# Low parts of the feed-forward weights, made for two units in one subtraction

## The reference

```python
h = h + mix
u = rms_norm(h, norm_mlp_g[i])
h = h + jnp.square(jax.nn.relu(u @ mlp_w1[i])) @ mlp_w2[i]
gate = jax.nn.sigmoid(rms_norm(h, ple_norm_g[i]) @ ple_w_gate[i])
h = h + gate * (p[i] @ ple_w_proj[i])
```

## Time and profile before

| | us |
|---|---|
| median of 3 runs | 1205.45 |
| lowest, highest run | 1203.81, 1205.74 |
| span of the profiled execution | 1202.4 |
| TensorE busy in it | 1190.7 (99%) |
| VectorE busy in it | 735.9 (61%) |
| ScalarE busy in it | 590.9 (49%) |

### The profile page before, as it was taken

One profiled execution on the slowest core, in us unless ns is written; L12 is line 12 of the kernel. 1 busy time (PEld: TensorE's weight loads), 2 busy tenths in 40 slices (PEclk: granted clock), 3 DMA queues, 4 the chain that ended last, 5 costly groups with the idle time before them and its releaser, 6 DMA issues.

```text
span 1202.4 us, 14118 instructions
## 1 busy us (share of the span) xinstructions
PE 1190.7 (99%) x5468; PEld 987.3 (82%) x5468; DVE 735.9 (61%) x977; ACT 590.9 (49%) x808; POOL 71.2 (6%) x63
## 2 busy tenths in 40 slices
PE   8999999999999999999999999999999999999998
PEld 6887788888888888888888888888888888888886
DVE  5677746778766647554465555556555557576554
ACT  6655444666566544443444433445433445455443
POOL 1000000000000011100011100012000012000000
PEclk9999999999999999999999999999999999999999
DMA  9777764333358667766568665677755676786661
GB/s 336 278 214 248 221 200 137 119 106 117 108 167 267 216 208 228 257 225 194 194 212 259 226 213 192 193 247 237 235 193 194 210 240 212 253 263 199 214 205 54
DMA packets 110980, 249.25 MB, mean 207 GB/s; under 512 B 9665, under 2 KB 55745, under 8 KB 110913
## 3 DMA queue, kind: packets, MB, share of 16 engines
q1 hardware_dynamic: 110768, 248.34, 63.6%
q10 hardware_dynamic: 144, 0.01, 0.0%
HBM read 233.63 MB, written 14.68 MB: 207 GB/s over the span
## 4 chain that ended last, share of the span: by engine, by line
PE 94%; DVE 2%; ACT 1%; DMA 1%; SPq 1%; issue 0%; ACTq 0%
PE acc L1495 88%; PE sc L1638 1%; DMA x_raw<-in_x_cols_dram 1%; DVE w_split L997 1%; ACT s L734 1%; PE sc L1603 0%; PE tr L1555 0%; PE tr L1544 0%; PE sc L1544 0%; PE tr L1691 0%; PE tr L1690 0%; PE acc L1527 0%; ACT q_split L719 0%; PE tr L1673 0%; PE tr L1667 0%
## 5 line engine op out<-in xcount | busy, mean ns | idle before, releaser
L997 DVE TENSOR_TENSOR w_split<-w_raw,w_split 128x1024 fp32r<-128x1024 f32 x408 | 506.0, 1249 | 382.0 <-ACT w_split L632 381.4
L632 ACT ACTIVATE w_split<-w_raw 128x1024 fp32r<-128x1024 f32 x408 | 428.5, 1058 | 414.5 <-PE acc L1495 410.8
L1495 PE MATMUL acc<-w_split,a_hi 128*128 128x512 f32 x1916 | 594.7, 392 | 4.7 <-DVE w_split L997 3.1
L1495 PE MATMUL acc<-w_split,b_split 128*128 128x512 f32 x1920 | 440.9, 390 | 0.0
L1495 PEld LDWEIGHTS acc<-w_split,a_hi 128*128 128x128 f32 x1916 | 356.2, 188 | 81.1 <-issue 4.9
L1495 PEld LDWEIGHTS acc<-w_split,b_split 128*128 128x128 f32 x1920 | 359.4, 188 | 74.0
L1495 PE MATMUL acc<-w_split,a_lo 128*128 128x512 f32 x958 | 373.2, 390 | 0.0
L1495 PEld LDWEIGHTS acc<-w_split,a_lo 128*128 128x128 f32 x958 | 179.8, 188 | 37.9
L591 POOL TENSOR_TENSOR stage<-stage 128x512 f32<-128x512 f32 x32 | 49.5, 1567 | 560.3 <-ACT stage L640 560.3
L734 ACT ACTIVATE s<-s,nmx,q_scale 128x128 f32<-128x128 f32 (+1 forms) x64 | 34.2, 539 | 7.8 <-DVE nmx L1175 7.4
L640 ACT ACTIVATE stage<-acc,rstd 128x512 f32<-128x512 f32 x48 | 30.2, 679 | 10.1 <-PE acc L1495 9.7
(11 more groups left out here) (184 smaller groups left out, 516.3 us busy)
## 6 DMA issues: line engine op xcount, KB each, us to landing
w_raw<-in_mlp_w_units_dram SPq DMA_DIRECT2D x256, 512.0 KB, 4.3
w_raw<-in_nsa_w_in_units_dram SPq DMA_DIRECT2D x76, 512.0 KB, 4.4
w_raw<-in_nsa_w_out_units_dram SPq DMA_DIRECT2D x32, 512.0 KB, 4.3
w_raw<-in_ple_w_gate_units_dram SPq DMA_DIRECT2D x32, 512.0 KB, 4.3
turn_dram<-s SPq DMA_DIRECT2D x52, 128.0 KB, 4.1
turn_dram<-junk SPq DMA_DIRECT2D x44, 128.0 KB, 4.2
v_slc<-turn_dram SPq DMA_DIRECT2D x22, 256.0 KB, 4.3
v_win<-turn_dram SPq DMA_DIRECT2D x22, 256.0 KB, 4.2
```

What stands on the lines that cost most here:

```text
L632: nc.scalar.activation(w_hi[:, u % SPLIT], w_raw[:, u % RAW], ACT.Copy).then_inc(hi_done, 1)
L997: nc.vector.tensor_tensor(w_lo[:, u % SPLIT], w_raw[:, u % RAW], f32(w_hi[:, u % SPLIT]), ALU.subtract).then_inc(lo_done, 1)
L1495: last = nc.tensor.matmul(acc[c % 2][t][:], xs[:, kt, toks], ws[:, u % SPLIT, m * NW:(m + 1) * NW], start=(kt == 0 and n == 0), stop=(kt = ...
```

## The change

A second generator, `split_lo_wide`, takes the place of `split_lo` in chunks 1 to 5 of all four quarters and in chunks 6 to 8 of the first three. At every even k it waits until the high parts of units k and k+1 are both done, subtracts both in one instruction of 2048 columns (the two slots lie side by side), and counts `lo_done` up by 2. At odd k it issues nothing. The other work stands behind the same k as before. Everything else, the last chunks of the last quarter among it, keeps `split_lo`.

```diff
+            def split_lo_wide(first, n, i=0):
+
+                for k in range(n):
+                    u = first + k
+                    if k % 2 == 0:
+                        dve.wait_ge(hi_done, u + 2 + 8 * UPC * i)
+                        s, r = slice(u % SPLIT, u % SPLIT + 2), slice(u % RAW, u % RAW + 2)
+                        nc.vector.tensor_tensor(w_lo[:, s], w_raw[:, r], f32(w_hi[:, s]),
+                                                ALU.subtract).then_inc(lo_done, 2)
                     yield k
 
@@ -1415,20 +1426,20 @@
             def hidden_chunks(i):
 
                 for j in range(1, 5):
-                    for k in split_lo(FIRST[C_MLP + j], UPC, i):
+                    for k in split_lo_wide(FIRST[C_MLP + j], UPC, i):
                         if k == 2 and j > 1:
                             turned_hidden(j - 2, i)
                         if k == 4:
                             dve.wait_ge(squared, TT * j + 4 * TT * i)
                             turn_blocks(T_HID + j - 1, lambda t: stage[:, t], i)
-                for k in split_lo(FIRST[C_MLP + 5], UPC, i):
+                for k in split_lo_wide(FIRST[C_MLP + 5], UPC, i):
                     if k == 2:
                         turned_hidden(3, i)
 
             for q in range(QUARTERS - 1):
                 hidden_chunks(q)
                 for j in range(6, 9):
-                    for k in split_lo(FIRST[C_MLP + j], UPC, q):
+                    for k in split_lo_wide(FIRST[C_MLP + j], UPC, q):
                         if j == 6 and k in (1, 2):
                             add_to_h(C_MLP + 3 + k, k - 1, q)
```

More of the change, by code:

```diff
@@ L999, in split_lo @@
                     yield k
+            def split_lo_wide(first, n, i=0):
[6 more added lines that the diff above has]
+                                                ALU.subtract).then_inc(lo_done, 2)
+                    yield k
             def transposed_lo(r, hi, lo, kt0, gain, i=0, banks=(0, 1)):
```

## The result

| | us |
|---|---|
| before, median of the runs | 1205.37 |
| after, median of the runs | 1226.79 |
| after / before | 1.0186 (95%: 1.0172 to 1.0199) |
| span of the profiled execution, before and after | 1202.4, 1225.9 |

A forecast was written before the change was run, and what follows sets the result against it. TensorE was taken as the bound, with no waits to win back. Its new stalls summed to 4.10 + 4e a quarter, 6.5 us with e = 0.6, 26 us in four quarters: 1205.45 + 26 = 1231.5 us, range 1212 to 1250.

The forecast's parts named there:

- The bound: Feed-forward part: TensorE has no slack and waits for nobody, VectorE has slack; TensorE busy 1190.7 of 1202.4 us.
- the 17 us of the working: VectorE's relief from 116 wide subtractions replacing 232: 0.15 us a pair, 17 us in all, none reaching the end.
- The pair's duration and slack: Wide subtraction takes about 2.30 us; low part ready at 6.11 against limit 7.72, leaving 1.6 us in an undisturbed pair.
- A - 6.31: Chunks 2 to 4: TensorE's stall at units 2 and 3, the block's return time in the chunk less 6.31 us.
- A - 7.85: Chunk 5, without evacuation or squaring: TensorE's stall is the block's return time in the chunk less 7.85 us.
- T: Moment SP sends the hidden block away to DRAM; forecast 18.32 us into chunk 1, 2.0 later than before.
- A to T: Chunks 2 to 4: from the block's return from DRAM to the next block's sending away, forecast 11.70 us.
- e: Lengthening of T to A because loads come in pairs; taken as 0.6 us, between near 0 and 1.6.
- T to A: Block's trip through DRAM, from sending away to return; 10.58 to 13.18 us before, forecast to lengthen by e.
- the prediction's own sign of being wrong: One of three signs: the block's return does not move though T, its sending away, does.
- Where the longest stall is: TensorE's longest idle time at unit 2 was forecast in chunk 2 of each quarter, about 3 us.
- a rival with 16 falls: TensorE's clock halves for one unit at each of 16 stalls: 43.5 us more, 1275 us; chance 0.04.

## Why the prediction was right

- **The bound.** TensorE was full in this stretch and VectorE was not: right. VectorE lost 30.5 us of work and the time rose. The relief was larger than the 17 us of the working, because squaring and subtracting now overlap less: GpSimd's squares fell from 1567 to 1042 ns on average, and 10 us of the relief lie in the subtractions for the turned blocks, which fell from 29.6 to 19.4 us in all.
- **The pair's duration and slack.** 2.29 undisturbed (2.30 forecast), 2.63 to 2.64 beside the squares (2.71). Pairs 0 and 1, 4 and 5, 6 and 7 and all of chunks 1 and 6 to 8 never stall, as forecast.
- **The limit.** A - 6.31 held: 1.08 by it, 1.12 in the stall shown, and within some 0.1 us in the others of chunks 2 to 4 (with the clock's 2.5 taken off the longest). A - 7.85 for chunk 5 gives 0.73 and 0.79 where the trace has 0.86 and 0.93.
- **The block's departure.** T was forecast at 18.32 in chunk 1 and is 613.33 - 595.03 = 18.30. A to T was forecast at 11.70 and is 11.43; VectorE's instructions overlap by some 0.08 at three places, which the sum leaves out, and that makes most of the difference.
- **The term that was mis-sized: e, and its spread.** T to A, by chunk from which the block comes: 12.19, 11.06, 10.91, 11.47 before, 11.16, 11.59, 12.43, 12.88 after. The mean e is 0.60, the value taken, and by the table above it lies on the way back (5.3 to 6.0). That the mean hit is in part luck, since 0.6 was a choice between 0 and 1.6: e is -1.0 for the first block of a quarter and +0.5, +1.5 and +1.4 for the others. So chunk 2 stalls 1.4 us on average where 3.0 were forecast, chunk 3 1.3 (1.1), chunk 4 2.2 (1.6), chunk 5 0.5 (0.75): 5.4 a quarter in place of 6.5. Why the first block travels faster than before is open; the moves of SP's order show what loads cost a block, not this.
- **The first block's arrival.** After chunk 1, T moved by 1.98 in every quarter, as forecast, but A in chunk 2 moved by -0.14, 0.69, 1.98 and 1.29. In the first quarter the prediction's own sign of being wrong, that A does not move though T does, was there, and ScalarE's wait in the second grew by 0.7 (2.91 to 3.61) and not by 2 to 3. Chunk 2 of the first quarter stalls all the same, because its old arrival (7.74) was past the new limit already.
- **Where the longest stall is.** Forecast in chunk 2; it is in chunk 4 of the second quarter, where T to A was 14.35.
- **The clock.** It had a chance of 0.04 as a rival with 16 falls. One fall came in the profiled execution, 2.5 us, and it makes the forecast seem closer than its stalls were (21.6 against 26).
- **What was not seen.** The sum had the round in it (18.01 - 6.31 is the 11.70 from A to T, so in chunks 3 and 4 the limit cancels and the round less 21.76 is left), but the prediction did not read it so, and the expectation for the evacuation went wrong by it: not the place of the pair but the length of the round decides from the second stall on.

## What to carry over

Merging two instructions into one saves some time on its engine (here 2 x 1.225 - 2.29 = 0.16 us), and makes the first half wait for the second half's input; count the second at the places where that input is late for another reason. Look for rounds: when a step's result comes back through several engines and DRAM to release the same step one iteration later, compare the round's length with the bound engine's iteration. Before, it was 11.08 + 11.4 = 22.5 against 21.76, already too long: in the first quarter A went from 7.74 in chunk 2 to 8.77 in chunk 5, and only slack and the end of the quarter hid it. The cure here was to send the block away and fetch it earlier in the order, not to make any step faster.

## What had not been expected of the hardware

The clock fell after stalls shorter than the 3.82 us of the changed kernel: in the kernel that fetches back sooner it was at 0.65 in the 4 us after a stall of 1.89 us. With only units 2 and 3 as pairs, 11 stalls of up to 1.71 us left it at full. In the kernel that subtracts twice it fell after 13 of 20 stalls: after two of 2.01 us, but not after the two others of that length, nor after one of 3.47. So the length of a stall alone does not say whether the clock falls, and runs of one kernel differ by it: with the evacuation behind unit 3, the shortest took 1219.88 us at a mean granted clock of 1.000, the longest 1224.84 at 0.996.
